# The eighth recurrent head of a layer also feeds four pieces of the second attention head's first projection unit

## What is computed

```python
for l in range(2):
    u = rmsnorm(h, norm_g[l])
    p = u @ w_in[l]                               # 1024 x 9216
    hq, hf_f, hf_b, hi, hgt, aq, ak, av, agt = split(p)
    o_h = hgrn2_mixer(hq, hf_f, hf_b, hi, hgt)    # 8 recurrent heads, both directions
    o_a = diff_attention_mixer(aq, ak, av, agt)   # 8 differential attention heads, rotary
    h = h + concatenate([o_h, o_a]) @ w_out[l]    # 2048 x 1024
out = rmsnorm(h, final_norm_g)[:, 16:]
```

## Time and profile before

| | before |
|---|---|
| median of three runs | 1385.91 us |
| profiled execution | 1386.22 us |
| its span, first to last instruction | 1384.4 us |
| outside the span | 1.8 us |
| TensorE busy | 1369.9 us (99%), 13108 matmuls |
| TensorE weight loads | 1291.0 us (93%) |
| VectorE busy | 1046.2 us (76%) |
| ScalarE busy | 837.3 us (60%) |
| GpSimd busy | 186.0 us (13%) |
| granted TensorE clock | 0.999 |

### The profile page before, as it was taken

The page is one execution under the profiler, slowest core; times in us unless marked ns, Lnnn a source line. Parts: engine busy times, 40 slices in busy tenths (PEclk is TensorE's granted clock), DMA queues, the critical chain, the costliest instruction groups (busy, mean ns, idle before and its releaser), DMA issues.

```text
span 1384.4 us, 32303 instructions
## 1 busy us (share of the span) xinstructions
PE 1369.9 (99%) x13108; PEld 1291.0 (93%) x13108; DVE 1046.2 (76%) x1765; ACT 837.3 (60%) x1802; POOL 186.0 (13%) x158
## 2 busy tenths in 40 slices
PE   9999999999999999999999999999999999999998
PEld 9999999998999999999998888888888899999987
DVE  6888887788646777877667888888886478888864
ACT  7666666666434666666555667666664456666654
POOL 1111222220000000000001122222210000000100
PEclk9999999999999999999999999999999999999999
DMA  5332322332323333333233232333323233334432
GB/s 188 117 98 93 108 85 86 108 108 78 99 71 122 101 99 100 103 90 100 70 107 108 87 106 85 108 107 108 108 82 108 85 110 107 108 107 114 114 96 76
DMA packets 76340, 140.41 MB, mean 101 GB/s; under 512 B 9504, under 2 KB 39456, under 8 KB 76192
## 3 DMA queue, kind: packets, MB, share of 16 engines
q1 hardware_dynamic: 76192, 138.35, 33.0%
HBM read 112.36 MB, written 17.30 MB: 94 GB/s over the span
## 4 chain that ended last, share of the span: by engine, by line
PE 89%; DVE 5%; ACT 2%; issue 2%; DMA 0%; SPq 0%; DVEq 0%; ACTq 0%
PE proj L1926 64%; PE far L2191 5%; PE pair L2174 3%; PE pair L2176 3%; PE far L2208 2%; PE pair L2059 1%; PE far L2193 1%; PE far L2144 1%; PE far L2145 1%; PE pair L2124 1%; DVE ops L1660 1%; PE pair L1926 1%; PE pair L2131 1%; DVE w_lo L1392 1%; PE far L2148 1%
## 5 line engine op out<-in xcount | busy, mean ns | idle before, releaser
L1926 PE MATMUL proj<-u_hi,w_hi 128*128 128x264 f32 (+1 forms) x1960 | 478.7, 312 | 1.9 <-DVE w_lo L1392 0.7
L1926 PE MATMUL proj<-u_lo,w_hi 128*128 128x264 f32 (+1 forms) x1960 | 458.2, 302 | 0.0
L1926 PE MATMUL proj<-u_hi,w_lo 128*128 128x264 f32 (+1 forms) x1960 | 458.1, 302 | 0.0
L1926 PEld LDWEIGHTS proj<-u_hi,w_hi 128*128 128x128 f32 x1960 | 314.7, 189 | 19.3 <-issue 1.4
L1926 PEld LDWEIGHTS proj<-u_hi,w_lo 128*128 128x128 f32 x1960 | 314.0, 188 | 13.6
L1926 PEld LDWEIGHTS proj<-u_lo,w_hi 128*128 128x128 f32 x1960 | 314.0, 188 | 10.6
L1392 DVE TENSOR_TENSOR w_lo<-w_raw,w_hi 128x1024 fp32r<-128x1024 f32 x178 | 221.9, 1247 | 35.9 <-ACT w_hi L952 35.8
L1200 ACT ACTIVATE decay<-pair,neg_max 128x528 f32<-128x528 f32 (+1 forms) x144 | 100.3, 697 | 203.4 <-DVE neg_max L1782 203.3
L952 ACT ACTIVATE w_hi<-w_raw 128x1024 fp32r<-128x1024 f32 x178 | 186.5, 1048 | 39.4 <-PE proj L1926 36.6
L1782 DVE TENSOR_REDUCE neg_max<-pair 128x1 f32<-128x528 f32 (+1 forms) x144 | 101.4, 704 | 90.5 <-PE pair L2176 89.3
L892 POOL TENSOR_TENSOR mix_lo<-mixed_t,mix_hi 128x528 fp32r<-128x528 f32 (+1 forms) x32 | 50.9, 1590 | 502.0 <-ACT mix_hi L1247 502.0
(11 more groups left out here) (257 smaller groups left out, 2245.7 us busy)
## 6 DMA issues: line engine op xcount, KB each, us to landing
w_raw<-w_units SPq DMA_DIRECT2D x178, 512.0 KB, 3.6
v_scratch<-blocks SPq DMA_DIRECT2D x128, 64.0 KB, 2.1
v_rows<-v_scratch SPq DMA_DIRECT2D x32, 256.0 KB, 2.9
o_scratch<-blocks SPq DMA_DIRECT2D x104, 64.0 KB, 2.7
q_stack<-gate_f SPq DMA_DIRECT2D x32, 132.0 KB, 2.4
k_stack<-k_stack SPq DMA_DIRECT2D x32, 132.0 KB, 2.4
o_rows<-o_scratch SPq DMA_DIRECT2D x14, 256.0 KB, 3.8
ops<-o_scratch SPq DMA_DIRECT2D x12, 256.0 KB, 2.6
```

The costliest lines, as they stand in the source:

```text
L1926: ins = pe.matmul(out, w, x[:, tile, cols_n], start=(k == 0 and p == 0), stop=(k == last_k and p == 2))
```

## The change

A constant and two lines. Head 7 (`HG_HEADS - 1`) gets the first four of head 8's pieces behind its own, and head 8 (`HG_HEADS`) leaves them out.

```diff
+AHEAD = 4
+
+
 def own_pieces(c):
@@ def fed_pieces(c):
     own = own_pieces(c)
     left = own_pieces(c - 1)[-carried(c - 1):] if c > 0 and carried(c - 1) else []
-    return left + own[:len(own) - carried(c)]
+    ahead = own_pieces(c + 1)[:AHEAD] if c == HG_HEADS - 1 else []
+    return left + own[AHEAD if c == HG_HEADS else 0:len(own) - carried(c)] + ahead
```

## The result

| | before | after |
|---|---|---|
| median | 1386.21 us (7 runs, 1385.78 to 1386.75) | 1391.50 us (7 runs, 1389.68 to 1392.46) |
| profiled execution, span | 1386.22, 1384.4 | 1389.68, 1387.9 |
| ratio after to before | | 1.0036, 95% interval 1.0024 to 1.0047 |

The forecast was 1385.0 with a range up to 1387.4; the range and the likeliest case are both missed. The runs of after fall in two groups, 1389.7 to 1390.1 and 1391.5 to 1392.5; the profiled one is of the lower group, and 3.5 us above the profiled one of before.

What follows compares the result with a forecast made beforehand. TensorE bounds the kernel, busy 1369.9 of 1384.4 us; VectorE paces the end of head 7. Gains of 0.57 and 0.60 less 0.3 in head 8 give 0.87 off 1386.22; median 0.3 lower: 1385.0 us, range 1382.0 to 1387.4.

Steps and rivals of the forecast that it cites:

- the likeliest case: The forecast of 1385.0 us itself, with a range of its own from 1383.9 to 1386.0; chance 0.76.
- (a): Head 7 to the last blend: blend only 0.1 and 0.2 us later, level matmuls' wait of 0.9 or 1.2 gone.
- The rival of the late transfers: SyncE's load, moved ahead of the stack's four transfers, delays head 8's scores: 1.6 us lost, 1386.6 us; chance 0.11.
- Step (b): Unit 42's evacuation, blocks and low cut, now ahead of head 7's forward chain, make L2144 2.36 and 2.18 us later.
- Step (c): Unit 43's rise and low cut around head 7's step 12 and head 8's first row maximum: nothing, at most 0.5 us.
- head 8: Its units start sooner: a bank wait of 0.15 us at unit 46, twice 0.3 in all, otherwise no change.
- the late gate: Head 8's gate of `ag` stays in step 2, TensorE waits 2.4 us instead of 0.23 per layer: 1389.4 us; chance 0.05.
- The first rival: Head 7's waits, 4.9 us together, go and nothing takes their place: 1381.0 us; chance 0.08.

Runs made afterwards that it cites:

- s5: Changed kernel with head 7's shares altered: two pieces go from ahead of step 5's level matmuls to behind them, same landings; 1386.96 us.
- b_s5: Kernel before with only head 7's shares altered: two of its 35 pieces go behind step 5's matmuls, landings kept; 1386.38 us, ratio 1.0000.
- s5_cut: Changed kernel with both the shares of s5 and the later cuts and load of cut_late; 1382.68 us.
- again: Changed kernel run once more with no edit; 1389.76 us, ratio 1.0028.
- cut_late: Changed kernel with unit 42's weight cuts and SyncE's load one step later, its evacuation and blocks staying in step 10; 1385.87 us.
- load_late: Changed kernel with SyncE's load of unit 47's weights in step 11 behind the stack's four transfers, instead of step 10; 1388.18 us.
- tail: Changed kernel with head 7's first 35 pieces in the steps of the kernel before and the four new ones all in step 12; 1394.41 us.
- turn: s5_cut with the second half of unit 41's turn in step 9 behind the last blend, instead of step 8; 1381.99 us.
- best2: The kernel best with 1 piece in step 11 and 4 in step 12, so unit 44 begins in step 12; 1384.37 us.
- best: Changed kernel with another head 7 table, as before ahead of step 5, three more pieces between steps 5 and 10, units 40 to 42 landing as before; 1391.69 us.

## Why the prediction was wrong

**The sum by its own steps.** Measured on TensorE against the kernel before, with the difference of the two traces ahead of head 7 taken off (-0.28 us in the first layer, +1.04 in the second; L2121 stands at 336.63 for 335.19, and at 1028.33 for 1025.91): the turn of the keys came 1.72 us later in the first layer and 1.39 in the second, where 0.1 and 0.2 were forecast. That is 2.8 too much. From there to the output of head 7 it is 2.20 and 1.92 us more, where the forecast has 2.26 and 1.98. The late transfers cost 0.3 and 1.2, counted to the end of the scores that wait for them. So -0.9 + 2.8 + 1.5 = +3.4 us, and 1386.22 + 3.4 = 1389.6; the profiled run has 1389.68. That it fits so well is partly luck: the -0.3 ahead of head 7 and a wait of 0.3 for a transfer in a later head of the second layer stand in no step of the forecast, and cancel. The upper group adds 2.4.

**The step that failed is (a)**, in the sentence "The level matmuls are reached 3 x 0.733 = 2.2 us later while their queries come hardly later", and "Net the blend and all that follows come +0.1 us". I counted the pieces ahead of steps 8, 10 and 12, and not those ahead of step 5; I asked what the level matmuls wait for, and not who waits for the level matmuls. The releaser in the earlier trace rows is ScalarE's copy, and I took its lateness for ScalarE's order of work alone, since evacuation and cut stood directly ahead of it. It had a second condition, the end of the group of matmuls that reads its buffer, only just met: the last of them start at 320.35 and last 0.46, and the copy starts at 320.95. Once two pieces stand ahead of them, it is this condition that sets the time: the loop goes from TensorE to ScalarE to VectorE, the queries and TensorE again. s5 shows it by taking just these two pieces away (2.8 us less), b_s5 shows the other condition, and s5_cut gives back the +0.1. With the two pieces, VectorE's stretch to the last blend is 1.61 us longer; the term had +0.1.

**The rival of the late transfers came true**, and had 0.11. Its price was right, 1.6 us forecast for 1.5 measured, and its mechanism in the main. In it the stack's bytes move only when the load has landed: load issued, 3.6 us for it, 3.0 for the stack. From the load's issue at 1034.69 that gives 1041.3, and they landed at 1036.87 + 4.32 = 1041.19. But the stack's bytes don't wait for the landing: their first packet starts at 1037.53, when most of the load's 128 packets are done, the load's last packet ends at 1038.54, and the first transfer of the stack lands at 1039.39 beside the load (1039.44). The load itself took 4.75 us instead of 3.6. The rule of the Trainium skill, "DMA: Bandwidth & Descriptors", section "Queues, rings and completion order", that the descriptors of one issuing engine are taken in ring order, agrees with the trace here; in the upper group (5.48 us) the last transfer lands 1.1 later than even this, as told under `again`. What I held against it (engines a third busy, two transfers that overlap) was a mean over stages: in the stretch from 1036 to 1040 us of `again` the DMA engines are busy for 0.96 of it.

**Step (b) was right**, as far as it goes: 2.2 and 1.9 us more ahead of the output, by the evacuation, the blocks and the low cut. Only the place of the loss is another, because part of the wait was already paid at the turn of the keys. cut_late and load_late price the two cuts together at 2.3 us in both layers, for 2.36 in the rows of the low cut. The other half, evacuation and blocks (1.38), was not taken out by itself.

**Step (c) and head 8 were right.** But for the transfers no wait over 0.1 us is new there in after; tail shows that the late gate's price of 2.2 to 2.4 was real, but its condition wasn't met, since the units land sooner. The first rival (the waits go, nothing takes their place, 1381.0) is what turn comes near, with 1381.99, after three edits.

**Left open:** whether all runs of the upper group have packets of the stack behind one of the instruction queue, as the one profiled does; and how much of the 3.6 us of s5_cut would come without the four pieces moved. b_s5 has only the shares and wins nothing, but the later cuts alone weren't tried in the kernel before.

## What to carry to other kernels

When work is put ahead of an instruction that waits, look not only at what it waits for but at who waits for it, buffer reuse included; a wait that has one releaser in the profile may have a second condition that is met a tenth of a microsecond sooner. Move the pieces and choose the shares of the steps together: by the shares alone the same 39 pieces gave 1384.4 (best2) to 1394.4 us (tail). And a transfer that the critical path needs shouldn't stand, on one issuing engine, behind a load that waits for something else.

## What of the hardware was not expected

- Four transfers of 132 KB behind a 512 KB load on SyncE's queue: the last lands 3.8 to 5.5 us after its issue, without the load ahead 2.4.
- In `again` one packet of the instruction queue (16384 bytes, 1.19 us) ended just where the last two packets of the stack began, and the transfer landed 1.1 us later than in after. As far as these two traces show, this is what the upper group has.
- A wait of 2.2 us was followed by some 3 us at a granted clock of 0.50 (1.2 GHz), which cost another 1.5 us. The two waits of 2.4 us in tail and those of 3.0 and 4.0 us in best also brought the clock down to 0.50. Waits of 1.0 to 1.7 us were not followed by a lower clock in any run. In the kernel best, behind its 4.0 us wait (busy time and count of the five engines from TensorE on, then granted clock, DMA share, GB/s):

```profile
1036.00:1045.00 9.00, 8.25 (x35) 7.59 (x36) 3.02 (x4) 1.90 (x10) 0.00 (x0) 0.63 0.32 90
```

The mean clock over these 9 us is 0.63.
